# Routed experts regrouped by load: three of the eight share one last group, the rest run one by one

## The reference

```python
logits = x @ w_router + b_router                 # 256 tokens x 8 experts
top_v, top_i = lax.top_k(logits, 2)              # two experts per token
top_w = softmax(top_v)
out = sum over e of gate[:, e] * ((silu(x @ w1[e]) * (x @ w3[e])) @ w2[e])
```

## Time and profile before

| What | Value |
|---|---|
| median of three executions | 2608.65 us (2607.48 to 2612.46) |
| span of the profiled execution | 2614.8 us |
| PE busy | 2393.3 us, 92% |
| DVE, ACT, POOL busy | 768.2, 643.7, 584.2 us |
| loads of expert weights | 189 of 2048 KB |
| bytes moved | 565.77 MB, 216 GB/s over the span |

### The profile page before, as it was taken

One profiled execution on the slowest core, in us unless ns is written; L12 is line 12 of the kernel. 1 busy time (PEld: TensorE's weight loads), 2 busy tenths in 40 slices (PEclk: granted clock), 3 DMA queues, 4 the chain that ended last, 5 costly groups with the idle time before them and its releaser, 6 DMA issues. The chain is left out here.

```text
span 2614.8 us, 61998 instructions
## 1 busy us (share of the span) xinstructions
PE 2393.3 (92%) x28274; PEld 1509.7 (58%) x28274; DVE 768.2 (29%) x1363; ACT 643.7 (25%) x974; POOL 584.2 (22%) x362
## 2 busy tenths in 40 slices
PE   4999898779999999698798779999999999999995
PEld 3776677547777778487577654444444444444443
DVE  2237765542222222615765430000000000000002
ACT  1243454332222222325455320100000000000001
POOL 4232542323333443234544300000000000000000
PEclk9999799889999999999799889999999999999997
DMA  7542001336435353231001289999999999999981
GB/s 252 193 161 77 3 4 36 99 130 218 161 129 177 113 181 109 65 121 41 6 4 36 66 325 390 402 400 397 398 401 402 399 397 401 398 372 387 404 348 55
DMA packets 205438, 565.77 MB, mean 216 GB/s; under 512 B 7856, under 2 KB 83008, under 8 KB 199552
## 3 DMA queue, kind: packets, MB, share of 16 engines
q1 hardware_dynamic: 193920, 528.63, 53.9%
q10 hardware_dynamic: 10112, 29.02, 3.4%
q0 software_dynamic: 1152, 4.19, 0.4%
HBM read 540.72 MB, written 21.10 MB: 215 GB/s over the span
## 5 line engine op out<-in xcount | busy, mean ns | idle before, releaser
L701 PE MATMUL bank<-arena 128*32 128x512 f32 (+1 forms) x6624 | 803.4, 557 | 5.9 <-issue 4.8
L311 POOL TENSOR_TENSOR w_lo<-arena,w_hi 128x2048 fp32r<-128x2048 f32 x78 | 354.2, 4542 | 627.0 <-ACT w_hi L305 626.9
L704 PE MATMUL bank<-arena 128*32 128x256 f32 (+1 forms) x6624 | 479.3, 361 | 0.0
L704 PEld LDWEIGHTS bank<-arena 128*32 128x32 f32 x6624 | 215.4, 110 | 435.5 <-issue 410.8
L321 PE MATMUL bank<-h_hi,w_hi 128*128 128x512 f32 (+1 forms) x1008 | 392.0, 389 | 48.1 <-DVE h_lo L1225 42.2
L322 PE MATMUL bank<-h_lo,w_hi 128*128 128x512 f32 (+1 forms) x1008 | 377.2, 374 | 0.0
L323 PE MATMUL bank<-h_hi,w_lo 128*128 128x512 f32 (+1 forms) x1008 | 377.0, 374 | 0.0
L701 PEld LDWEIGHTS bank<-arena 128*32 128x32 f32 x6624 | 208.7, 110 | 125.6 <-issue 10.7
L321 PEld LDWEIGHTS bank<-h_hi,w_hi 128*128 128x128 f32 x1008 | 195.2, 194 | 113.5 <-issue 61.9
L514 POOL DMA_INDIRECT arena<-slot_y,arena x4 | 3.8, 951 | 1028.6 <-ACTq L567 1027.7
L640 DVE TENSOR_TENSOR arena<-arena,bank 128x768 f32<-128x768 f32 (+2 forms) x45 | 31.3, 713 | 664.1 <-ACT arena L542 664.1
(11 more groups left out here) (262 smaller groups left out, 2521.5 us busy)
## 6 DMA issues: line engine op xcount, KB each, us to landing
arena<-in_moe_w_dram SPq DMA_DIRECT2D x189, 2048.0 KB, 12.2
arena<-in_w_mod_dram SPq DMA_DIRECT2D x48, 1024.0 KB, 5.0
arena<-in_ffn_w_dram SPq DMA_DIRECT2D x42, 1024.0 KB, 7.0
arena<-in_w_in_dram SPq DMA_DIRECT2D x26, 1024.0 KB, 6.3
arena<-in_w_out_dram SPq DMA_DIRECT2D x8, 1024.0 KB, 9.6
slot_x<-arena ACTq DMA_DIRECT2D x1, 4992.0 KB, 26.3
slot_y<-arena ACTq DMA_DIRECT2D x1, 4992.0 KB, 55.7
x_store<-arena ACTq DMA_DIRECT2D x2, 2048.0 KB, 6.5
```

The lines of the kernel that those rows point to most:

```text
L311: pool.tensor_tensor(lo, slot_view(splits[i][0]), hi, ALU.subtract).then_inc(sem("w_lo"), 1)
L701: mm(bank[b][64 * h + 32 * c:64 * h + 32 * c + 32, 0:n // 2], xa[:, 32 * c:32 * c + 32], w[:, n // 2 * h:n // 2 * (h + 1)], start=first, s ...
L704: ins = mm(bank[b + 1][blk(q), 0:n // 4], xb, w[:, n // 4 * q:n // 4 * (q + 1)], start=first, stop=last)
```

## The change

The experts are ranked: expert 0 first, then the others by falling number of tokens. Rank 0 gets 96 slots, rank 1 gets 192, ranks 2 to 5 get 96, and ranks 6 and 7 get 32 each. What is above an expert's slots goes to extra items of 96. The items are then rank 0, ranks 2 to 5, and the extra items, each computed as before. With the numbers of tokens above there are no extra ones: experts 0, 5, 7, 2 and 1 are items 0 to 4. After them comes one group of three: A is rank 1 (161 tokens in 192 slots), B and C are ranks 6 and 7 (21 and 18 tokens). Each of the three experts is loaded once, through the same ring.

In the group a row of A's weights is met by twelve matmuls of half the row (`wide`, three banks), and a row of B's or C's by four of a quarter (`narrow`). In chunk s the order is: w2 of B and then of C for chunk s-1; for each unit of w1 and then of w3 the unit of A, of B and of C in turn; transposes of A's gate; w2 of A for chunk s; transposes of B's and C's gates. w1, w3 and the turned gate share one place in the banks (0 to 2 for A, 3 for B and C); outputs are in 4 to 6 and in 7.

DVE's chain for the routing gets longer, POOL fills a table with 24 small memsets, and the rows cleared in each slot array are 1344 in place of 1248. PE starts item 0 without the table of items, and reads its register after it; SP loads all of item 0 without it. On PE items 0, 1 and 2 are written out, then a loop from 3 to the last but one, then the last and the group of three.

```diff
+    NI = 5 + 6
+    CAP_A, CAP_B = 192, 32
+    S_AT = NI * SLOTS
...
+        trio_order = []
+        for s in range(NC + 1):
+            runs = [("w2", who, s - 1) for who in "BC"] + [("w1", "A", s), ("w3", "A", s), ("w2", "A", s)]
+            for kind, who, s_ in runs:
+                if 0 <= s_ < NC and kind == "w2":
+                    trio_order += [(who,) + u for u in units_of(kind, s_)]
+                elif s_ < NC and who == "A":
+                    for u in units_of(kind, s_):
+                        trio_order += [(x_,) + u for x_ in "ABC"]
+        trio_place = {u: j for j, u in enumerate(trio_order)}
...
+        def trio_psum(g, n):
+
+            if g == "A":
+                return ps[:, 0:3, 0:n // 2]
+            return pk(3, 2, 256)[:, :, 0:n // 4]
+
+        def trio_sbuf(tiles, g, n):
+            return tiles[g][:, :, 0:n // (2 if g == "A" else 4)]
...
+            def load_trio(e, i, j):
+                sp.wait_ge(sem("m_unit"), NU * i + (NU + j - MRING + 1))
+                sp.sem_inc(sem("m_turn"), 1)
+                u = trio_order[j]
+                sp.dma_start(ring_slot(j, u[1:]), rows_of(e[u[0]], u[1:])).then_inc(sem(f"slot{j % MRING}"), 16)
...
             sp.wait_ge(sem("out_mm"), KD * L)
             for j in range(MRING):
                 load(None, None, j)
+            for j in range(MRING, NU):
+                load(None, 0, j)
             sp.wait_ge(sem("items"), 1)
-            last = sp.value_load(it_i[0:1, 2 * NI:2 * NI + 1], min_val=NE - 1, max_val=NI - 1)
-            with sp.Fori(0, last) as i:
+            last = sp.value_load(it_i[0:1, NI + 3:NI + 4], min_val=4, max_val=NI - 1)
+            e1_ = sp.value_load(it_i[0:1, 1:2], min_val=0, max_val=NE - 1)
+            for j in range(MRING):
+                load(e1_, 1, j)
+            with sp.Fori(1, last) as i:
...
+            three_e = {x: sp.value_load(it_i[0:1, NI + n:NI + n + 1], min_val=0, max_val=NE - 1)
+                       for n, x in enumerate("ABC")}
+            for j in range(len(trio_order)):
+                load_trio(three_e, last, j)
+            sp.wait_ge(sem("m_ys"), last + 3)
+            trio_results(sp, "A", range(6))
+            sp.wait_ge(sem("m_ys"), last + 4)
+            trio_results(sp, "C", range(4))
...
+            def item_trio(i):
+                for s in range(NC):
+                    trio_sig(i, "A", s)
+                    trio_sig(i, "BC", s)
+                    trio_turned(i, "A", s)
+                    trio_turned(i, "BC", s)
+                for j, g in enumerate(("A", "BC")):
+                    act.wait_ge(sem("m_unit"), NU * i + (NU + trio_last(g, "w2", NC - 1) + 1))
+                    act.activation(YSS[g], trio_y(g), ACT.Copy).then_inc(sem("m_ys"), 1)
+                act.wait_ge(sem("m_ys"), i + 4)
+                trio_results(act, "B", range(4))
...
+            count = it_n[:, 2]
+            link(nc.vector.tensor_copy(count, pk(3, 3, NE)[:, 2]))
+            link(stt(out=rank, in0=pk(3, 3, NE)[:, 0:2], scalar=1.0, in1=chosen, op0=ALU.add, op1=ALU.mult))
+            link(ts(rank, rank, -1.0, None, ALU.add))
             for t in range(2):
                 ins = ts(SEL[:, t], io[:, 0:SLOTS], rank[:, t, 0:1], None, ALU.is_equal)
             ins.then_inc(sem("m_sel"), 1)
...
+            cap, base = it_n[:, 0], it_n[:, 1]
+            for n in range(2):
+                link(tt(picked, by_rank, tabs[:, 1 + n:2 + n, :].to_broadcast(sq), ALU.mult))
+                link(reduce_(it_n[:, n], picked))
+            link(tt(count, count, cap, ALU.subtract))
+            link(ts(over[:, 0], count, 0.0, None, ALU.is_gt))
+            link(stt(out=over[:, 0], in0=count, scalar=float(SLOTS), in1=over[:, 0], op0=ALU.is_gt, op1=ALU.add))
...
+            def wide(b, n, x64, w, first, last_):
+
+                for h in range(2):
+                    for c in range(2):
+                        ins = mm(bank[b][64 * h + 32 * c:64 * h + 32 * c + 32, 0:n // 2], x64[:, 32 * c:32 * c + 32],
+                                 w[:, n // 2 * h:n // 2 * (h + 1)], start=first, stop=last_)
+                return ins
+
+            def narrow(dst, n, x32, w, first, last_):
+
+                for q in range(4):
+                    ins = mm(dst[blk(q), :], x32, w[:, n // 4 * q:n // 4 * (q + 1)], start=first, stop=last_,
+                             skip_group_check=True)
+                return ins
...
+            def hidden_trio(i, x, kind, s, part):
+                n, g = CHUNKS[s][1], "A" if x == "A" else "BC"
+                k = part * unit_rows((kind, s, 0))
+                if kind == "w3":
+                    pe.wait_ge(sem("m_s"), NC * i + (NC + trio_nth(g, s) + 1))
+                elif s:
+                    pe.wait_ge(sem("m_gt"), NC * i + (NC + trio_nth(g, s - 1) + 1))
+                for u in trio_units(x, kind, s)[part:part + 1]:
+                    j = trio_place[u]
+                    wait_trio(i, j)
+                    for r in range(unit_rows(u[1:])):
+                        w = ring_slot(j, u[1:])[:, r]
+                        if x == "A":
+                            for b in range(3):
+                                ins = wide(b, n, XGS[:, k, 64 * b:64 * b + 64], w, k == 0, k == KD - 1)
+                        else:
+                            ins = narrow(trio_psum(g, n)[:, x == "C"], n, XGS[:, k, row0[x]:row0[x] + CAP_B], w,
+                                         k == 0, k == KD - 1)
+                        k += 1
+                    ins.then_inc(sem("m_unit"), 1)
...
+                pe.wait_ge(sem("m_xg"), 2 * i + 6)
+                for s in range(NC):
+                    if s:
+                        down_trio(i, "B", s - 1)
+                        down_trio(i, "C", s - 1)
+                    for kind in ("w1", "w3"):
+                        for part in range(len(units_of(kind, s))):
+                            for x in "ABC":
+                                hidden_trio(i, x, kind, s, part)
+                    turn_trio(i, "A", s)
+                    if s == 0:
+                        pe.wait_ge(sem("m_ys"), i + 2)
+                    down_trio(i, "A", s)
+                    turn_trio(i, "BC", s)
+                down_trio(i, "B", NC - 1)
+                down_trio(i, "C", NC - 1)
...
+            item(0, True)
             pe.wait_ge(sem("items"), 1)
-            last = pe.value_load(it_i[0:1, 2 * NI:2 * NI + 1], min_val=NE - 1, max_val=NI - 1)
-            for i in range(NE - 2):
+            last = pe.value_load(it_i[0:1, NI + 3:NI + 4], min_val=4, max_val=NI - 1)
+            for i in (1, 2):
                 item(i, True)
-            with pe.Fori(NE - 2, last) as i:
+            with pe.Fori(3, last) as i:
                 item(i, True)
             item(last, False)
...
+            caps = [SLOTS, CAP_A] + 4 * [SLOTS] + 2 * [CAP_B]
+            bases = [0, S_AT] + [SLOTS * i for i in range(1, 5)] + [S_AT + CAP_A, S_AT + CAP_A + CAP_B]
+            keys = [BIG] + list(range(NE - 2, -1, -1))
+            for i, row in enumerate((keys, caps, bases)):
+                for e in range(NE):
+                    ins = nc.gpsimd.memset(tabs[:, i, e:e + 1], float(row[e]))
+            ins.then_inc(sem("iota"), 1)
```

More of the change, by code:

```diff
@@ L404, in hybrid_kernel @@
         io = table(P)
[L405 to L408, removed]
+        tabs = table(3, NE)
+        key = table(NE)
+        order_of = table(NE)
+        by_rank = table(NE, NE)
+        picked = table(NE, NE)
+        it_n = table(6, NE)
+        over = table(2, NE)
+        it_f = table(NI + 4)[0:1]
+        it_i = table(NI + 4)[0:1].bitcast(i32)
         XTK = area(o_mix, 2, D)
@@ L554, in item @@
                 act.wait_ge(sem("m_ys"), i + 1 + 1)
-                results(act, i, range(2), range(4 if more else 0))
+                results(act, i, range(2), range(4))
             act.sem_inc(sem("m_yo"), 1)
@@ L565, in moe_act @@
             item(last, False)
-            act.wait_ge(sem("m_yo"), 96 * last + 97)
+            item_trio(last)
+            act.wait_ge(sem("m_yo"), 96 * last + (97 + 16 * 14))
             act.sem_inc(sem("slot_y"), 1)
@@ L651, in moe_dve @@
             item(last)
+            item_trio()
             for t in range(2):
@@ new lines, in turn_trio @@
+            def turn_trio(i, g, s):
+                n = CHUNKS[s][1]
+                pe.wait_ge(sem("m_g"), NC * i + (NC + trio_nth(g, s) + 1))
+                src, dst = trio_sbuf(SG, g, n), trio_psum(g, n)
+                for b in range(3 if g == "A" else 2):
+                    for f in range(n // (256 if g == "A" else 512)):
+                        ins = nc.tensor.transpose(dst[:, b, f * P:(f + 1) * P], src[:, b, f * P:(f + 1) * P], ident)
+                ins.then_inc(sem("m_tr"), 1)
@@ new lines, in down_trio @@
+            def down_trio(i, x, s):
+                n, f, g = CHUNKS[s][1], 0, "A" if x == "A" else "BC"
+                nf = n // (256 if x == "A" else 512)
```

(15 more changed lines are left out.)

144 lines of the change are left out of this document (111 added, 33 removed).

## The result

The changed kernel takes 2467.73 us (median of four, 2465.14 to 2473.34), the one before 2610.56 us (four, 2607.48 to 2613.18): ratio 0.9456, 95% interval 0.9441 to 0.9471. The recorded execution has a span of 2464.8 us, 150.0 less than the recorded one of before; the medians are 142.8 apart. The prediction was 2467, from -141.2.

What follows compares the result with a forecast made beforehand. PE was taken to set the pace, the ring staying supplied by a thin margin. Removing all behind item 4 (-457.7), then + 315.8 - 0.8 + 1.2 + 0.3, gave -141.2 from 2608.65: 2467 us, range 2456 to 2498.

Steps and rivals of the forecast that it cites:

- What bounds: Kernel before: PE sets the pace and the ring stays supplied, but the margin is thin and the change spends it.
- The group: Group of three after item 4: products, narrow rows, transposes, new waits and waits for loads, 315.8 us in all.
- the 2 us for matmuls of 128 columns: B's and C's last chunk: 32 rows of 128 columns cost 0 to 6.9 us beyond column time, taken as 2.
- Rival 4: B's and C's products: narrow's four tiles don't overlap when alone, 217 us more, 2684; chance 0.03.
- New waits of PE: Group: PE waits newly because the banks are shared, taken as 9.4 us, bounds 6 to 14.
- (c): A's w3 needs A's sigmoid and product, 3.3 us; last w1 units of B and C cover it with 3.44; taken as nothing.
- (d): Group: A's gate product is covered by B's and C's w3 units alike.
- Does the ring hold?: Group: ready units run out in the last chunk; PE waits for loads, taken as 5 us at about 398 GB/s.
- rival 2: Group: PE's clock falls at the new waits, 2.7 us each, 22 to 30 in all, 2489 to 2497; chance 0.14.
- The start: Routing ahead of item 0: DVE's chain before the selection matrix falls from seven small operations to three, -0.8 us.
- The end: Output writes after the group: A's six issues run into SP's four, ACT's copy is shorter, +0.3 us.
- rival 1: Group: the transfer becomes the bound, 8 us longer at 390 GB/s, 31 at 380; chance 0.18 for above 2480.

Runs made afterwards that it cites:

- half loads: Each load in the group brings only the first half of its unit, products unchanged, against the changed kernel: 2461.89 us, group 306.7.
- The narrow chunk first: The chunk of 512 comes first and not last, in items and group, against the changed kernel: 2467.28 us, group 310.6.
- the repeats: The changed kernel run again twice, unedited: 2470.49 and 2467.30 us.
- the order by expert: In the group w1 and w3 go all units of A, then B, then C, against the changed kernel: 2470.99 us beside 2470.49.
- two light units first: Changed kernel with B's and C's transposes ahead of A's w2, and the group's first triple in order B, C, A: 2465.48 us.
- B and C alone: Later part of a run with the group as all of A, then B and C together, against the changed kernel's mixed order: 2606.95 us.
- the two bracketing runs: Against the changed kernel, group loads cut to their first half: 2461.89 us; or about three in eight of B's and C's products computed: 2466.30 us.

## Why the prediction was right

*What bounds.* That PE set the pace with a ring in store, and that the group would spend it, holds: waits for loads only in the second half, 4.7 us in all, all in the last 100 us.

*The group*, 315.8 predicted, 313.8 measured. With half loads it is 306.7, of which 8.4 are waits on ACT, so products and transposes are 298.3. I had 301.4. The largest error is the 2 us for matmuls of 128 columns: with half loads, 16 such rows stand between these two starts.

```profile
2382.97 3.68 PE L940 MATMUL bank<-arena 128*32 128x128 f32 x128
2386.46 10.54 PE L933 MATMUL bank<-arena 128*32 128x256 f32 x192
```

3.49 / 16 = 0.218 us, beside 0.215 by columns. My range was 0.215 to 0.43, and the low end was right: eight instructions in 0.218 us, 27 ns apart, cost next to nothing. Rival 4 falls with it, and for narrow rows of 256 columns as well: in the same recording B's unit starts in two triples that follow each other are 13.75 us apart (2120.68 and 2134.43), four wide rows at 2.58 and eight narrow ones at 0.43.

*New waits of PE*: 9.4 predicted, 8.4 measured (1.5 and 1.6 a time, not 1.75). The covers of (c) and (d) held: no wait on DVE in the group.

*Does the ring hold?* The size was right, 5 against 4.7, by a reason that was wrong in part. I had taken one rate, about 398, and said that at 410 PE would wait for nothing. The rate is 408 for rows of 4 KB and 385 to 390 for the last chunk's 2 KB. An average over an item hid that, and in the group the slow units come just when the store is lowest. The narrow chunk first shows it. The lulls were there, some 5 us of transfer and not 8.

*The clock* (rival 2, 0.14): right in kind, small in size. The waits of 0.7 to 1.6 us leave it at 1.00. Behind the one of 3.1 us it is at 0.50 for some 3 us, which costs 1.3; 2.8 and 2.9 in the repeats. What a wait of this length costs differs from run to run: in the order by expert one of 2.8 us is followed by 1.7 us of lower clock, and with two light units first one of 3.2 us leaves the clock at 1.00. I had priced none into the forecast.

*The start*: -0.8 predicted, -2.3 measured. The wait for the selection matrix fell from 2.07 to 1.25 us, which is the -0.8. The rest is PE's gather of item 0, which took 7.04 us before:

```profile
1535.66 5.41 PE L1017 MATMUL bank<-arena 128*128 128x96 f32 x32 [1.25 <-DVE arena L722]
```

It is no chance of one execution: the gather takes 5.41 us in all twelve recordings with the new routing that I can compare (the changed kernel and its edits), and 7.04 in both with the old one. Before, the clock is at 0.50 in each us from 1543 to 1549; after, it is near 1.00 in the first us, at 0.50 from 1537 to 1540, and near 1.00 again behind that. So the shorter wait goes with a shorter stretch at the lower level, worth 1.6 us, a term that the forecast didn't have; why the stretch is shorter stays open. *PE's register read* cost nothing: items 0 and 1 end 112.5 apart. *The end*: +0.3 predicted, +1.5 measured, of which 0.7 lie ahead of POOL's first gather. SP's writes are why:

```profile
2417.20 4.79 SPq L566 DMA_DIRECT2D slot_y<-arena  x6
2422.10 1.94 SPq L569 DMA_DIRECT2D slot_y<-arena  x4
```

A's six took 4.8 us to issue and not 3.4, so C's four start 1.9 us behind the copy. The other half lies behind the gather's start, and I haven't traced it.

*The sum with what was measured*: -457.7 + 313.8 - 2.3 + 1.1 + 1.5 = -143.6, and -142.1 with the 315.3 of a repeat. The medians are 142.8 apart, so nothing is left for the 6.4 us ahead of the routing.

*The page on HBM.* The Trainium skill's "DMA: Bandwidth & Descriptors" (Specifications) has about 358 GB/s for one core; with B and C alone, where PE is busy for only 53 of 100 us, the rate is 409 over these 100 us. The measurement decides.

*The transfer as the bound* (rival 1) was nearer than its 0.18 says. The two bracketing runs put its limit at 308.6 and PE's at 306.7. That the time came out right to a microsecond owes something to luck: the errors in the group were +3.1 (products and transposes), +1.0 (waits on ACT), +0.3 (waits for loads) and -2.4 (the clock and what has no place), with -3.7 for the last in a repeat; outside it the start was 1.5 too small and the end 1.2, which cancel; and the first recording's stretch ahead of the experts is no part of the sum.

## What to carry to other kernels

Before merging work to save loads, write down for each piece its compute and its transfer: here 10.3 against 5.1 us a unit for the heavy expert, 1.7 against 5.1 for the light ones. With the same loads and products the change was worth 5 us when the pieces ran one after another (the loop's 8 included), and 143 when heavy and light were mixed so that both sums came out alike; up to 36 us of the difference are waits that the mixed order covers for the most part, and the clock behind them. When two limits lie within 3% of each other, further small savings on one of them are handed to the other: cut each alone, leaving work out, before tuning either.

## What the runs showed of the hardware

- One load stream of 2 MB units runs at about 408 GB/s with rows of 4 KB, and at 385 to 390 with rows of 2 KB.
- In four column tiles fp32 matmuls of 128 columns alone keep column time, 0.218 us for a row of four (eight instructions).
- A jump back of PE's loop over some 1500 matmul instructions cost 4.8 us of standing and 2.7 of lower clock; with one more pass written out (no jump back) both are gone. The loops of SP, ACT and DVE over the same items cost nothing that shows in the 112.5 us between the ends of items.
- In the group the granted clock stayed at 1.00 through waits of 0.7 to 1.6 us. Behind single waits of 2.8 to 3.3 us it fell to 0.50 for a few us in five recordings, which cost 1.3 to 2.9 us each, and in a sixth it did not fall.
- The same gather of 32 matmul instructions took 7.04 us behind a wait of 2.07 us and 5.41 behind one of 1.25, in each recording; the granted clock was 0.50 in nearly all of the first and for some 3 us of the second.
